# Gathering an expert's tokens as rows through a resting selection, then turning them, in a two-layer encoder with a mixture of experts

## The chip, the core and the metric

The kernel runs on one core of one Trainium2 chip. The metric is the device time of one execution in microseconds (us), which the chip itself measures. Three executions of the kernel before took 1951.26 to 1951.74 us, with a median of 1951.43 us. Lower is better.

## What is computed

The program is two encoder layers over 256 tokens of width 1024. Each layer has a mixer (retention, RWKV-7, latent attention) and a feed-forward block. The change lies in the second layer's feed-forward block, which is a mixture of eight experts where each token takes its two best ones:

```python
def swiglu(h, wg, wu, wd):
    return (jax.nn.silu(h @ wg) * (h @ wu)) @ wd

def moe_swiglu(h, router, wg, wu, wd):
    logits = (h @ router).astype(jnp.float32)
    top_v, top_i = lax.top_k(logits, TOP_K)          # TOP_K = 2
    top_w = jax.nn.softmax(top_v, axis=-1)
    comb = jnp.sum(jax.nn.one_hot(top_i, N_EXPERTS, dtype=jnp.float32) * top_w[..., None], axis=-2)
    out = jnp.zeros(h.shape, jnp.float32)
    for e in range(N_EXPERTS):                       # 8 experts, 1024 -> 3584 -> 1024
        out = out + comb[..., e:e + 1] * swiglu(h, wg[e], wu[e], wd[e]).astype(jnp.float32)
    return out.astype(h.dtype)
```

All inputs and weights are float32. `h` is the hidden state after an RMS norm with a gain per channel.

## The kernel before

**Items.** Each expert is worked off as one "item" of a hardware loop that all engines run in step, eight times here. An item takes at most 128 tokens: a 0/1 matrix `sel` (tokens x slots, two tiles of 128 tokens) picks them. Three weight matrices stream through a ring of three slots (`ring`, 2 MB each). A slot holds two halves, and a half is the unit of work; `q` counts the 42 halves of an item. Halves 0 to 27 are the gate and up matrices (`eg0`, `eu0`, ... `eg6`, `eu6`, two halves each), halves 28 to 41 the down matrix.

**Splitting.** To multiply float32 data at the speed of the rounded float32 type (fp32r), each operand is split in a high and a low part, and three products are summed. For each half the scalar engine (ACT) copies it from the ring into `w_hi` (L1003), the vector engine (DVE) subtracts that from the ring to give `w_lo` (L1677, a helper that all its two-input operations share), and TensorE (PE) does 12 matmuls of 128x128 by 128x512 (L1611). There are three buffers for such halves (PARTS), so ACT may begin half q only when PE has used up half q - 3. The order on each engine is the order of the code.

**Jobs and banks.** What PE writes goes to eight PSUM banks. The products of an item are a list, `ITEM`, with the engine that reads each one out. A job's bank is its place in that list modulo 8, and PE may begin a job only when the job eight places ahead of it in the list has been read out:

```python
def item_bank(job):
    k = ITEM_AT[job]
    if k >= BANKS:
        item_read_out(ITEM[k - BANKS][0])
```

In the list before, places 22 and 23 are `eg6` (read by ACT) and `eu6` (read by DVE), 24 and 25 are `eT5` and `eT6`, 26 and 27 are `gx0` and `gx1`, 28 and 29 are `ed0` and `ed1`. `ed0` and `ed1` are the two accumulators of the down matrix; PE asks for both banks just before half 28, behind `turn(5)`, four transposes of the activation (L1622). DVE reads `eu6` with one multiplication (`ehm`) that its code puts behind its work on half 29.

**The gather.** For each item the chosen tokens have to stand as columns, channel by channel, in `xg_hi` and `xg_lo`. PE makes them straight from the normed rows `hn` (two tiles of 128 tokens by 1024 channels), 16 full float32 matmuls of 128 columns with `hn` as the resting operand and `sel` moving (L1559), behind half 32, into `gx0` and `gx1`. ACT (L975) and DVE (L2167) scale and split them behind half 35, for the item that comes next. The first item's gather stands ahead of the loop, where it waits for `hn` and for `sel`, which DVE makes at the end of the routing (compare the logits, rank them, L1677 and its neighbours). After that come dummy products that keep PE busy, and the loop.

**GpSimd** (POOL) has nothing to do in this part but one load.

Of the kernel before, what the change touches and what calls it, by code (L numbers as in the profile page):

```python
# [11 lines left out]
F32 = mybir.dt.float32  # L12
I32 = mybir.dt.int32
ALU = mybir.AluOpType
# [3 lines left out]
P = 128  # L18
# [165 lines left out]
def moe_jobs():  # L184

    A, V = "act", "vec"
    out = [("eg0", A)] + [(f"sc{u}{t}", V) for u in range(2) for t in range(T)] + [("csT", A), ("eu0", V)]
    for j in range(1, 7):
        out += [(f"eg{j}", A), (f"eu{j}", V), (f"eT{j - 1}", V)]
    out += [("eT6", V), ("gx0", V), ("gx1", V), ("ed0", V), ("ed1", V)]  # L190
    return out


# [20 lines left out]
ITEM = moe_jobs()  # L214
ITEM_AT = {n: i for i, (n, _) in enumerate(ITEM)}
PANELS = panels()
AHEAD = 4
EP = 21
HALVES = 14 + 13
SURE = NE  # L220
# [34 lines left out]
class Signals:  # L255


    def __init__(self, nc):
        new = nc.alloc_semaphore
        self.ident_loaded = new("ident_loaded")  # L260
        self.const_loaded = new("const_loaded")
        self.pos_loaded = new("pos_loaded")
        self.mu_loaded = new("mu_loaded")
        self.vec_loaded = new("vec_loaded")
        self.first_gain_loaded = new("first_gain_loaded")
        self.gain_loaded = new("gain_loaded")
        self.router_loaded = new("router_loaded")
        self.fgain_loaded = new("fgain_loaded")
        self.i_hi_ready = new("i_hi_ready")
        self.i_lo_ready = new("i_lo_ready")  # L270
        self.i_half_used = new("i_half_used")
        self.i_x_hi_ready = new("i_x_hi_ready")
        self.i_x_lo_ready = new("i_x_lo_ready")
        self.f_hi_ready = new("f_hi_ready")
        self.f_lo_ready = new("f_lo_ready")
        self.f_half_used = new("f_half_used")
        self.f_x_hi_ready = new("f_x_hi_ready")
        self.f_x_lo_ready = new("f_x_lo_ready")
        self.hi_ready = new("hi_ready")
        self.lo_ready = new("lo_ready")  # L280
        self.half_used = new("half_used")
        self.x_hi_ready = new("x_hi_ready")
        self.product_ready = new("product_ready")
        self.freed_act = new("freed_act")
        self.freed_vec = new("freed_vec")
        self.act_step = new("act_step")
        self.vec_step = new("vec_step")
        self.pool_step = new("pool_step")
        self.out_stored = new("out_stored")
        self.angles_ready = new("angles_ready")  # L290
        self.trig_ready = new("trig_ready")
        self.sumsq_ready = new("sumsq_ready")
        self.var_ready = new("var_ready")
        self.root_ready = new("root_ready")
        self.factor_ready = new("factor_ready")
        self.hn_ready = new("hn_ready")
        self.shift_zero = new("shift_zero")
        self.xs_ready = new("xs_ready")
        self.lora_act_ready = new("lora_act_ready")
        self.knsq_ready = new("knsq_ready")  # L300
        self.knroot_ready = new("knroot_ready")
        self.decay_sig_ready = new("decay_sig_ready")
        self.rate_sig_ready = new("rate_sig_ready")
        self.logd_ready = new("logd_ready")
        self.exps_ready = new("exps_ready")
        self.cex_ready = new("cex_ready")
        self.scan_in_ready = new("scan_in_ready")
        self.rope_ready = new("rope_ready")
        self.silu_g_ready = new("silu_g_ready")
        self.gn_var_ready = new("gn_var_ready")  # L310
        self.gn_root_ready = new("gn_root_ready")
        self.ret_done = new("ret_done")
        self.qa_sumsq = new("qa_sumsq")
        self.qa_ready = new("qa_ready")
        self.mla_key_ready = new("mla_key_ready")
        self.masked_ready = new("masked_ready")
        self.prob_ready = new("prob_ready")
        self.merged_done = new("merged_done")
        self.blocks_ready = new("blocks_ready")
        self.x_ready = new("x_ready")  # L320
        self.state_ready = new("state_ready")
        self.rwkv_done = new("rwkv_done")
        self.y_pairs_done = new("y_pairs_done")
        self.route_exp = new("route_exp")
        self.route_diff = new("route_diff")
        self.mask_ready = new("mask_ready")
        self.items_ready = new("items_ready")
        self.sel_ready = new("sel_ready")
        self.ey_hi_ready = new("ey_hi_ready")
        self.fin_ready = new("fin_ready")  # L330
        self.items_done = new("items_done")


def build(nc, x, positions, attn_norm, w_in, rwkv_mu, rwkv_w0, rwkv_w2, rwkv_a0, rwkv_a2, rwkv_g2, rwkv_k_k,
# [5 lines left out]
    def sb(name, shape, dt=F32, where=None):  # L340
        size = -(-int(np.prod(shape[1:])) * 4 // 32) * 32
        if where is None:
            where = at[0]
            at[0] += size
        return nc.alloc_sbuf_tensor_at(name, shape, dt, offset=where)
# [93 lines left out]
    xg_lo = sb("xg_lo", [P, KD, P], F32R, where=X + 53248)  # L439
    ehT_hi = sb("ehT_hi", [P, 28, P], F32R, where=X + 57344)  # L440
    ehT_lo = sb("ehT_lo", [P, 28, P], F32R, where=X + 71680)
    sel = sb("sel", [P, T, P], where=X + 86016)
    weight = sb("weight", [P, 2, T], where=X + 87040)
    selT = sb("selT", [P, SEQ], F32R, where=X + 88064)
    ehm = sb("ehm", [P, 2, 512], where=X + 89088)
# [37 lines left out]
    freed = {"act": s.freed_act, "vec": s.freed_vec}  # L483
    FR = {e: freed_count(len(JOBS) - 1, e) for e in freed}
    IF = {e: item_freed(len(ITEM) - 1, e) for e in freed}
    LOOP_FR = {"act": FR["act"], "vec": FR["vec"] + AHEAD}
    NPAN = len(PANELS)

    def product(eng, job):
# [69 lines left out]
    def factor(m, t):  # L559

        return stat[:, 0, T * m + t:T * m + t + 1]
# [82 lines left out]
    def _(pool):  # L644
# [50 lines left out]
                own.step(G.tensor_copy(mk[:, t, :, 64:96], each(qa[:, t, 384:416], NH)), s.mla_key_ready)  # L695
        read_out(pool, "o11.1")
        pool.dma_start(fgain[:], final_norm.partition_broadcast(P)).then_inc(s.fgain_loaded, 16)


    @block.scalar  # L700
    def _(act):
# [28 lines left out]
        for l in range(DEPTH):  # L730
# [205 lines left out]
            if l:  # L936
                for t in range(T):
                    act.wait_ge(s.factor_ready, T * (2 * l + 1) + t + 1)
                    own.step(A.activation(hn[:, t, :], h[:, t, :], ACT.Copy, scale=factor(2 * l + 1, t)), s.hn_ready)
            if l == 0:  # L940
                for q in range(2, 36):
                    ffn_high(q)
# [24 lines left out]
        act.wait_ge(s.route_diff, 1)  # L967
        own.step(A.activation(stat[:, 6, 0:2], stat[:, 6, 0:2], ACT.Exp), s.route_exp)

        def gathered_hi(eng_wait):  # L970

            for u in range(2):
                b = eng_wait(f"gx{u}")
                for i in range(4):
                    ins = A.activation(xg_hi[:, 4 * u + i, :], b[:, i * P:(i + 1) * P], ACT.Copy,  # L975
                                       scale=gains[:, 1, 1, 4 * u + i:4 * u + i + 1])
                ins.then_inc(s.x_hi_ready, 1)

        def down_hi(eng_wait):

            for u in range(2):
                A.activation(ey_hi[:, 512 * u:512 * u + 512], eng_wait(f"ed{u}")[:], ACT.Copy)\
                    .then_inc(s.ey_hi_ready, 1)

        gathered_hi(lambda job: ahead(act, job))
        act.wait_ge(s.items_ready, 1)
        n_items = act.value_load(items[0:1, 24:25], min_val=SURE, max_val=SURE + 3)
        with act.Fori(0, n_items) as item:
# [16 lines left out]
            for q in range(2 * EP):  # L1005
# [11 lines left out]
                if q % 4 == 1 and 9 <= q <= 33:  # L1017
# [2 lines left out]
                                 item_product(f"eT{j}")[:].rearrange("p (c n) -> p c n", c=4),  # L1020
                                 ACT.Copy).then_inc(s.x_hi_ready, 1)
                if q == 35:
                    gathered_hi(item_product)
        def last_product(job):
            act.wait_ge(s.product_ready, n_items * len(ITEM) + (len(JOBS) + AHEAD + ITEM_AT[job] + 1 - len(ITEM)))
# [11 lines left out]
    def _(pe):  # L1037
# [514 lines left out]
        def gather(b_of):  # L1552

            for u in range(2):
                b = b_of(f"gx{u}")
                for i in range(4):
                    for t in range(T):
                        n = 4 * u + i
                        ins = M(b[:, i * P:(i + 1) * P], hn[:, t, n * P:n * P + P], sel[:, t, :], start=t == 0,  # L1559
                                stop=t == T - 1)  # L1560
                done(ins)

        keep_on(banks[ITEM_AT["gx0"] % BANKS], 4)
        pe.wait_ge(s.hn_ready, T)
        pe.wait_ge(s.sel_ready, 1)
        gather(lambda job: banks[ITEM_AT[job] % BANKS])
        for u in range(2):
            keep_on(banks[ITEM_AT[f"ed{u}"] % BANKS], 8)
            done(M(banks[ITEM_AT[f"ed{u}"] % BANKS][:], ident, cst[:, 0:512], start=True, stop=True))
# [14 lines left out]
        with pe.Fori(0, n_items) as item:  # L1584
# [41 lines left out]
            for j in range(7):  # L1626
                for g, name in enumerate(("eg", "eu")):
# [11 lines left out]
                    if j == g == 0:  # L1639
                        scatter(item, item_bank)  # L1640
                        b = item_bank("csT")
                        for t in range(T):
                            ins = TR(b[:, t * P:(t + 1) * P], sel[:, t, :], ident)
                        done(ins)
                if j:
                    turn(j - 1)
# [1 line left out]
            for j in range(7):  # L1648
# [3 lines left out]
                for r in range(2):  # L1652
# [11 lines left out]
                    if q == 32:  # L1664
                        pe.wait_ge(s.sel_ready, item + 2)
                        gather(item_bank)
        scatter(n_items, lambda job: banks[ITEM_AT[job] % BANKS])


    @block.vector  # L1670
    def _(dve):
# [517 lines left out]
        with dve.Fori(0, n_items) as item:  # L2189
# [19 lines left out]
            for q in range(2 * EP):  # L2209
# [16 lines left out]
                if q % 4 == 2 and 10 <= q <= 34:  # L2226
# [2 lines left out]
                    dve.wait_ge(s.x_hi_ready, item * 9 + (j + 3))  # L2229
                    tt(ehT_lo[:, 4 * j:4 * j + 4, :], b[:].rearrange("p (c n) -> p c n", c=4),  # L2230
                       ehT_hi[:, 4 * j:4 * j + 4, :].bitcast(F32), ALU.subtract).then_inc(s.freed_vec, 1)
                if q == 35:
                    gathered_lo(item_product, item * 9 + 9)

        def final(job):
# [48 lines left out]
```

## Time and profile before

| | value |
|---|---|
| median of the runs | 1951.43 us |
| the profiled execution's own time | 1948.17 us |
| its span, first to last instruction | 1946.4 us |
| routing, first gather, start of the loop | 925 to 943.5 us of the span |
| loop of 8 items | 943.5 to 1933 us, about 123.6 us each |
| TensorE busy over the span | 98% |
| mean granted TensorE clock | 0.996 |

The profiled execution took 1.8 us more than its span, and 3.3 us less than the median of the runs. Records of matmuls overlap (one begins before the last one's record ends), so PE's pace is read from the starts of its instructions or from the chain of work, and not from the length of one.

### The profile page before, as it was taken

Reading aid. Unit: us, or ns where it says so; the run is one execution under the profiler, and the core shown is the slowest. Engines: PE = TensorE matmul, PEld = TensorE weight load, DVE = VectorE, ACT = ScalarE, POOL = GpSimd, SP = SyncE. Lnnn points to the kernel's source line nnn. Section 1 sums busy time; section 2 is a strip of 40 time slices with the busy share of each in tenths; the row PEclk is TensorE's granted clock in tenths of the full one; section 3 lists DMA queues with packets and bytes.
Section 4 is the critical chain, followed back from the end, with each engine's and each line's share of the span. In section 5 each row is a group of like instructions: output and inputs, shape, how many; then the busy total and the mean of one; then the engine's idle time right before and its main releaser. Section 6 shows DMA issues by size and latency. Waiting matters only on the chain.

```text
span 1946.4 us, 25957 instructions
## 1 busy us (share of the span) xinstructions
PE 1903.1 (98%) x10058; PEld 1462.0 (75%) x10058; DVE 1356.4 (70%) x1403; ACT 1116.6 (57%) x1097; POOL 99.5 (5%) x124
## 2 busy tenths in 40 slices
PE   8999999999999999999999999999999999999997
PEld 7865655688888755654888888888888888888886
DVE  5664445444546644452888998889889899888997
ACT  5555211433444563110777777777777777777775
POOL 1340000000000520000000000000000000000000
PEclk9999999999999999999999999999999999999999
DMA  9542132553557422221899999999999999998994
GB/s 327 186 157 87 45 131 88 208 188 130 216 182 221 145 94 80 88 94 42 325 369 346 357 370 339 369 343 358 369 341 366 346 361 362 343 369 344 361 374 157
DMA packets 181498, 485.65 MB, mean 250 GB/s; under 512 B 5880, under 2 KB 12660, under 8 KB 172600
## 3 DMA queue, kind: packets, MB, share of 16 engines
q1 hardware_dynamic: 176256, 475.40, 67.0%
q0 software_dynamic: 1488, 5.57, 0.8%
q10 hardware_dynamic: 3688, 3.74, 0.7%
q8 instruction: 48, 0.79, 0.2%
q14 instruction: 18, 0.15, 0.0%
HBM read 479.93 MB, written 1.05 MB: 247 GB/s over the span
## 4 chain that ended last, share of the span: by engine, by line
PE 95%; DVE 2%; ACT 2%; issue 1%; DMA 0%; SPq 0%; ACTq 0%; DVEq 0%
PE bank L1611 47%; PE bank L1092 19%; PE bank L1205 9%; PE bank L1084 7%; PE bank L1559 2%; PE bank L1255 1%; PE bank L1622 1%; PE bank L1580 1%; PE bank L1304 1%; DVE m L1677 1%; DMA ring<-w_in_dram 0%; PE bank L1281 0%; PE bank L1229 0%; PE bank L1171 0%; PE bank L1269 0%
## 5 line engine op out<-in xcount | busy, mean ns | idle before, releaser
L1677 DVE TENSOR_TENSOR w_lo<-ring,w_hi 128x2048 fp32r<-128x2048 f32 x336 | 765.1, 2290 | 112.4 <-ACT w_hi L1003 112.4
L1003 ACT ACTIVATE w_hi<-ring 128x2048 fp32r<-128x2048 f32 x336 | 643.7, 1916 | 126.3 <-PE bank L1611 126.2
L1611 PE MATMUL bank<-w_hi,xg_hi 128*128 128x512 f32 x896 | 353.0, 394 | 1.5 <-DVE w_lo L1677 1.5
L1611 PE MATMUL bank<-w_hi,xg_lo 128*128 128x512 f32 x896 | 349.7, 390 | 0.0
L1611 PE MATMUL bank<-w_lo,xg_hi 128*128 128x512 f32 x896 | 349.4, 390 | 0.0
L1611 PEld LDWEIGHTS bank<-w_hi,xg_hi 128*128 128x128 f32 x896 | 168.8, 188 | 36.1 <-DVE w_lo L1677 2.3
L1611 PEld LDWEIGHTS bank<-w_hi,xg_lo 128*128 128x128 f32 x896 | 168.2, 188 | 35.3
L1611 PEld LDWEIGHTS bank<-w_lo,xg_hi 128*128 128x128 f32 x896 | 168.4, 188 | 34.0
L1205 PE MATMUL bank<-ring,hnT 128*128 128x512 f32 x384 | 178.4, 600 | 0.0
L1611 PE MATMUL bank<-w_hi,ehT_hi 128*128 128x512 f32 x448 | 176.5, 394 | 0.0
L1611 PE MATMUL bank<-w_hi,ehT_lo 128*128 128x512 f32 x448 | 174.8, 390 | 0.0
L1611 PE MATMUL bank<-w_lo,ehT_hi 128*128 128x512 f32 x448 | 174.5, 390 | 0.0
L1677 DVE TENSOR_TENSOR ring_lo<-ring,f_hi 128x2048 fp32r<-128x2048 f32 (+1 forms) x36 | 75.4, 2111 | 76.6 <-ACT f_hi L922 76.6
L1677 DVE TENSOR_TENSOR ring_lo<-ring,i_hi 128x2048 fp32r<-128x2048 f32 (+2 forms) x36 | 79.6, 2219 | 68.0 <-ACT i_hi L743 68.0
L1205 PEld LDWEIGHTS bank<-ring,hnT 128*128 128x128 f32 x384 | 69.4, 190 | 63.9 <-issue 61.3
L1092 PE MATMUL bank<-i_hi,ix_hi 128*128 128x512 f32 (+2 forms) x288 | 110.3, 383 | 4.9 <-DVE ring_lo L1677 3.8
L1092 PE MATMUL bank<-ring_lo,ix_hi 128*128 128x512 f32 (+2 forms) x288 | 111.0, 385 | 0.0
L1092 PE MATMUL bank<-i_hi,ix_lo 128*128 128x512 f32 (+2 forms) x288 | 109.4, 380 | 0.0
L1611 PEld LDWEIGHTS bank<-w_hi,ehT_lo 128*128 128x128 f32 x448 | 84.1, 188 | 17.7
L1611 PEld LDWEIGHTS bank<-w_hi,ehT_hi 128*128 128x128 f32 x448 | 84.4, 188 | 16.8
L1611 PEld LDWEIGHTS bank<-w_lo,ehT_hi 128*128 128x128 f32 x448 | 84.2, 188 | 16.9
L1084 PE MATMUL bank<-ring,yT 128*128 128x512 f32 x192 | 85.5, 598 | 3.0 <-issue 3.0
(401 smaller groups left out, 2532.7 us busy)
## 6 DMA issues: line engine op xcount, KB each, us to landing
ring<-moe_w_gate_dram SPq DMA_DIRECT2D x56, 2048.0 KB, 7.8
ring<-moe_w_up_dram SPq DMA_DIRECT2D x56, 2048.0 KB, 8.0
ring<-moe_w_down_dram SPq DMA_DIRECT2D x56, 2048.0 KB, 8.4
ring<-w_in_dram SPq DMA_DIRECT2D x26, 2048.0 KB, 8.6
ring<-w_branch_dram SPq DMA_DIRECT2D x6, 2048.0 KB, 8.2
ring<-ffn_w_gate_dram SPq DMA_DIRECT2D x5, 2048.0 KB, 8.3
ring<-ffn_w_up_dram SPq DMA_DIRECT2D x5, 2048.0 KB, 8.1
ring<-ffn_w_down_dram SPq DMA_DIRECT2D x5, 2048.0 KB, 8.0
```

The costliest lines, as they stand in the source:

```text
L1003: A.activation(w_hi[:, q % PARTS, :], ring[:, i, o:o + HALF], ACT.Copy).then_inc(s.hi_ready, 1)
L1084: ins = M(b[:, 0:width], lhs[:, c, t * P:(t + 1) * P], w[:, c, c0:c0 + width], start=c == 0, stop=c == k - 1)
L1092: ins = M(dst, a[:, c, tok], v[:, cols], start=start and n == 0, stop=stop and n == 2, skip_group_check=True)
L1205: ins = M(dst[:], hnT[:, c, (g % 2) * P:(g % 2) * P + P], gates[0][:, 512 * c:512 * c + 512], start=c == 0, stop=c == KD - 1, skip_group_c ...
L1255: ins = M(b[ch, cols], left[ch, :], right[ch, :], start=True, stop=True)
L1304: ins = M(b[:, 256 * i:256 * i + 256], C("same_block"), rows_of[:, 2 * u + i, :], start=True, stop=True)
L1559: ins = M(b[:, i * P:(i + 1) * P], hn[:, t, n * P:n * P + P], sel[:, t, :], start=t == 0, stop=t == T - 1)
L1580: ins = M(b[:], selT[:, t * P:(t + 1) * P], part[:, 512 * u:512 * u + 512], start=i == 0, stop=i == 1)
L1611: ins = M(dst, a, w, start=start and n == 0, stop=stop and n == 2, skip_group_check=True)
L1622: ins = TR(b[:, c * P:(c + 1) * P], ehm[:, j % 2, c:512:4], ident)
L1677: return V.tensor_tensor(out_, a, b, op)
```

## The change

The selection becomes the resting operand and the token rows move. `hn` is split once ahead of the loop: ACT writes `hn_hi` (rounded to fp32r) beside `hn`, and POOL subtracts to give `hn_lo`. A gather is now 8 fp32r matmuls of 512 columns into two new jobs, `gy0` and `gy1`; ACT copies them to SBUF as rows (`xrow`); and behind half 35 PE turns them by 8 transposes of 128x128 into `gx0` and `gx1`. ACT's and DVE's scaling and splitting moves from half 35 to half 38. The list of jobs has 32 places in place of 30.

```diff
@@ moe_jobs
-    out += [("eT6", V), ("gx0", V), ("gx1", V), ("ed0", V), ("ed1", V)]
+    out += [("eT6", V), ("gy0", A), ("gy1", A), ("gx0", V), ("gx1", V), ("ed0", V), ("ed1", V)]
...
-AHEAD = 4
+AHEAD = 6
...
-    sel = sb("sel", [P, T, P], where=X + 86016)
+    sel = sb("sel", [P, T, P], F32R, where=X + 86016)
+    hn_lo = sb("hn_lo", [P, T, D], F32R, where=hn_at)
+    hn_hi = sb("hn_hi", [P, T, D], F32R, where=X + 113664)
+    xrow = sb("xrow", [P, D], where=X + 121856)
...
-    LOOP_FR = {"act": FR["act"], "vec": FR["vec"] + AHEAD}
+    LOOP_FR = {"act": FR["act"] + 2, "vec": FR["vec"] + AHEAD - 2}
@@ gpsimd, at its end
         pool.dma_start(fgain[:], final_norm.partition_broadcast(P)).then_inc(s.fgain_loaded, 16)
+        for t in range(T):
+            pool.wait_ge(s.hn_ready, 2 * t + 2)
+            G.tensor_tensor(hn_lo[:, t, :], hn[:, t, :], hn_hi[:, t, :].bitcast(F32), ALU.subtract)\
+                .then_inc(s.hn_lo_ready, 1)
@@ scalar
                     own.step(A.activation(hn[:, t, :], h[:, t, :], ACT.Copy, scale=factor(2 * l + 1, t)), s.hn_ready)
+                    own.step(A.activation(hn_hi[:, t, :], h[:, t, :], ACT.Copy, scale=factor(2 * l + 1, t)), s.hn_ready)
...
+        def gathered_rows(eng_wait):
+
+            for u in range(2):
+                A.activation(xrow[:, 512 * u:512 * u + 512], eng_wait(f"gy{u}")[:], ACT.Copy).then_inc(s.freed_act, 1)
+
...
+        gathered_rows(lambda job: ahead(act, job))
         gathered_hi(lambda job: ahead(act, job))
...
                 if q == 35:
+                    gathered_rows(item_product)
+                if q == 38:
                     gathered_hi(item_product)
@@ tensor
         def gather(b_of):
 
             for u in range(2):
+                b = b_of(f"gy{u}")
+                for t in range(T):
+                    for part in (hn_hi, hn_lo):
+                        ins = M(b[:], sel[:, t, :], part[:, t, 512 * u:512 * u + 512], start=t == 0 and part is hn_hi,
+                                stop=t == 1 and part is hn_lo)
+                done(ins)
+
+        def turn_gathered(b_of):
+
+            for u in range(2):
                 b = b_of(f"gx{u}")
                 for i in range(4):
-                    for t in range(T):
-                        n = 4 * u + i
-                        ins = M(b[:, i * P:(i + 1) * P], hn[:, t, n * P:n * P + P], sel[:, t, :], start=t == 0,
-                                stop=t == T - 1)
+                    n = 4 * u + i
+                    ins = TR(b[:, i * P:(i + 1) * P], xrow[:, n * P:n * P + P], ident)
                 done(ins)
 
-        keep_on(banks[ITEM_AT["gx0"] % BANKS], 4)
-        pe.wait_ge(s.hn_ready, T)
+        keep_on(banks[ITEM_AT["gy0"] % BANKS], 4)
+        pe.wait_ge(s.hn_lo_ready, T)
         pe.wait_ge(s.sel_ready, 1)
         gather(lambda job: banks[ITEM_AT[job] % BANKS])
+        pe.wait_ge(s.freed_act, LOOP_FR["act"])
+        turn_gathered(lambda job: banks[ITEM_AT[job] % BANKS])
...
                     if q == 32:
                         pe.wait_ge(s.sel_ready, item + 2)
                         gather(item_bank)
+                    if q == 35:
+                        item_read_out("gy1")
+                        turn_gathered(item_bank)
@@ vector
-                if q == 35:
+                if q == 38:
                     gathered_lo(item_product, item * 9 + 9)
```

**PE's program between halves 27 and 28, in the loop.** The rows below are PE's instructions in order: the end of `eu6` (in bank 7), the turn of `eT5` (in bank 0), and the first products of half 28. A register row carries the wait of the line of code behind it. Before:

```order
L1611 MATMUL bank7<-w_hi_127,xg_lo_130 128x512
L1588 REGISTER_ALU [waits freed_vec]
L1622 MATMUL bank0<-cst_56,ehm_136 128x128 [waits freed_act]
L1622 MATMUL bank0<-cst_56,ehm_136 128x128 x3
L1588 REGISTER_ALU [waits freed_vec]
L1615 REGISTER_ALU [waits freed_vec]
L1611 MATMUL bank4<-w_hi_127,ehT_hi_131 128x512 [waits lo_ready]
```

And now:

```order
L1639 MATMUL bank7<-w_hi_127,xg_lo_130 128x512
L1616 REGISTER_ALU [waits freed_vec]
L1650 MATMUL bank0<-cst_56,ehm_139 128x128 [waits freed_act]
L1650 MATMUL bank0<-cst_56,ehm_139 128x128 x3
L1616 REGISTER_ALU [waits freed_act]
L1643 REGISTER_ALU [waits freed_vec]
L1639 MATMUL bank6<-w_hi_127,ehT_hi_131 128x512 [waits lo_ready]
```

The down accumulators moved from banks 4 and 5 to banks 6 and 7, the banks of `eg6` and `eu6`; what is waited for there was `eu5` and `eT4`, and is now `eg6` and `eu6`.

**ACT's program ahead of the loop.** The rows are those from the norm of the last layer to the first gathered tokens, with `h` the hidden state. Before, two rows stood between the second square root and the routing's exponential, L939 `hn<-h,stat` twice. Now:

```order
L721 ACTIVATE stat<-stat 128x1 [waits var_ready]
L948 ACTIVATE hn<-h,stat 128x1024 [waits factor_ready]
L949 ACTIVATE hn_hi<-h,stat 128x1024
L948 ACTIVATE hn<-h,stat 128x1024 [waits factor_ready]
L949 ACTIVATE hn_hi<-h,stat 128x1024
L978 ACT_TABLE_LOAD
L978 ACTIVATE stat<-stat 128x2 [waits route_diff]
L983 ACTIVATE xrow<-bank 128x512 [waits product_ready] x2
L990 ACTIVATE xg_hi<-bank,gains 128x128 [waits product_ready]
```

Two copies of 1024 columns came in beside `hn`, and two of 512 columns ahead of `xg_hi`. POOL's new row, `L705 TENSOR_TENSOR hn_lo<-hn,hn_hi 128x1024 [waits hn_ready] x2`, is the last of its program.

## Rows read from the trace of the kernel before

**Rows 1.** The page: TensorE's busy time, share of span, instructions
```profile
PE 1903.1 (98%) x10058; PEld 1462.0 (75%) x10058; DVE 1356.4 (70%) x1403; ACT 1116.6 (57%) x1097; POOL 99.5 (5%) x124
```

**Rows 2.** Windows: us, each engine's busy us, PEclk, DMA share, GB/s
```profile
1062.00:1186.00 124.00, 124.00 (x577) 103.60 (x576) 110.07 (x76) 93.88 (x70) 0.00 (x0) 1.00 0.96 357
```

**Rows 3.** Waits from 950 to 1940: us in total, times, longest
```profile
ACT w_hi L1003 <- PE bank L1611: 125.4, 214, 1.6
...
PE bank L1580 <- DVE ey_lo L1677: 0.2, 1, 0.2
```

**Rows 4.** Chain that ended last, in order: start us, us, what
```profile
1024.64 0.47 PE bank L1622 x4
...
1148.24 0.47 PE bank L1622 x4
...
1154.67 8.22 PE bank L1611 x36
1162.89 3.57 PE bank L1559 x32
...
1196.41 1.82 PE bank L1580 x8
```

**Rows 5.** Timeline around half 28: start us, us, engine, instruction
```profile
1145.27 4.53 DVE L1677 TENSOR_TENSOR w_lo<-ring,w_hi 128x2048 fp32r<-128x2048 f32 x2 [0.40 <-ACT w_hi L1003]
...
1145.55 1.92 ACT L1003 ACTIVATE w_hi<-ring 128x2048 fp32r<-128x2048 f32 x1 [0.32 <-PE bank L1611]
...
1148.46 0.48 PE L1611 MATMUL bank<-w_hi,ehT_hi 128*128 128x512 f32 x1
1148.74 0.60 ACT L1019 ACTIVATE ehT_hi<-bank 128x512 fp32r<-128x512 f32 x1 [1.27 <-PE bank L1622]
...
1149.71 0.68 DVE L1677 TENSOR_TENSOR ehm<-bank,esg 128x512 f32<-128x512 f32 x1
```

**Rows 6.** Timeline behind half 35, the split of the gathered tokens
```profile
1164.75 1.12 ACT L975 ACTIVATE xg_hi<-bank,gains 128x128 fp32r<-128x128 f32 x4
...
1167.16 2.16 DVE L2167 SCALAR_TENSOR_TENSOR xg_lo<-bank,gains,xg_hi 128x128 fp32r<-128x128 f32 x8
```

**Rows 7.** Timeline ahead of the loop: routing, first gather, first half
```profile
925.38 2.17 ACT L939 ACTIVATE hn<-h,stat 128x1024 f32<-128x1024 f32 x2
...
927.66 0.29 DVE L1677 TENSOR_TENSOR higher<-rt 128x128 f32<-128x128 f32 x1
...
928.19 0.29 DVE L1677 TENSOR_TENSOR equal<-equal,cst 128x128 f32<-128x128 f32 x1
...
932.27 0.28 DVE L2113 TENSOR_SCALAR sel<-cst,spos 128x128 f32<-128x128 f32 x1
...
932.94 3.74 PE L1559 MATMUL bank<-sel,hn 128*128 128x128 f32 x32
...
936.71 1.14 ACT L975 ACTIVATE xg_hi<-bank,gains 128x128 fp32r<-128x128 f32 x4 [0.64 <-PE bank L1559]
...
943.46 0.50 PE L1611 MATMUL bank<-w_hi,xg_hi 128*128 128x512 f32 x1 [1.49 <-DVE w_lo L1677]
```

**Rows 8.** Timelines of POOL's and DVE's two-input operations in the mixer
```profile
81.63 2.78 POOL L657 TENSOR_TENSOR rope_tmp<-raw,cosT 128x256 f32<-128x256 f32 x1
...
83.73 1.76 DVE L1677 TENSOR_TENSOR prev<-prev,pr 128x1024 f32<-128x1024 f32 x1
...
91.17 0.74 POOL L656 TENSOR_TENSOR rope_tmp<-raw,cosT 128x256 f32<-128x256 f32 x1
...
134.97 0.46 POOL L655 TENSOR_TENSOR mrope_tmp<-mq,sinT 128x128 f32<-128x128 f32 x1
...
147.51 1.22 DVE L1677 TENSOR_TENSOR tmp<-y_ret 128x1024 f32<-128x1024 f32 x1
```

**Rows 9.** Windows with a lower granted clock, columns as above
```profile
925.00:930.00 5.00, 4.77 (x29) 4.77 (x30) 2.71 (x16) 3.56 (x4) 0.00 (x0) 0.68 1.00 357
...
1934.00:1938.00 4.00, 1.18 (x4) 0.65 (x4) 2.73 (x5) 1.86 (x4) 0.00 (x0) 0.89 0.00 0
```

More of the change, by code:

```diff
@@ L296, in __init__ @@
         self.hn_ready = new("hn_ready")
+        self.hn_lo_ready = new("hn_lo_ready")
         self.shift_zero = new("shift_zero")
@@ L441, in build @@
     ehT_lo = sb("ehT_lo", [P, 28, P], F32R, where=X + 71680)
-    sel = sb("sel", [P, T, P], where=X + 86016)
+    sel = sb("sel", [P, T, P], F32R, where=X + 86016)
+    hn_lo = sb("hn_lo", [P, T, D], F32R, where=hn_at)
+    hn_hi = sb("hn_hi", [P, T, D], F32R, where=X + 113664)
+    xrow = sb("xrow", [P, D], where=X + 121856)
+    assert X + 125952 <= int(nc.sbuf_usable_end)
     weight = sb("weight", [P, 2, T], where=X + 87040)
@@ L1642, in _ @@
                         for t in range(T):
-                            ins = TR(b[:, t * P:(t + 1) * P], sel[:, t, :], ident)
+                            ins = TR(b[:, t * P:(t + 1) * P], sel[:, t, :].bitcast(F32), ident)
                         done(ins)
```

## The prediction

> **What bounds the kernel now.** I read the page first: TensorE (PE) is busy for 98% of the span [rows 1]. Then the windows of the loop: in an item of 124 us PE is busy for all of it, DVE for 110 and ACT for 94, the clock is full, and the DMA engines are 0.96 busy [rows 2]. Busy PE alone proves little, so the table of waits comes next: over the eight items ACT waits 125 us for PE to free a split buffer, and PE itself waits once, for 0.2 us [rows 3]. So the loop goes at PE's pace, and what PE does in an item counts in full, eight times. The chain of work prices it: from one turn of `eT5` to the same one an item later it is 1148.24 - 1024.64 = 123.6 us; 36 products of 512 columns take 8.22 us, or 0.228 each; 8 such products of another kind take 1.82; a turn of four transposes takes 0.47; and the gather, 32 passes for 16 float32 matmuls, takes 3.57 [rows 4].
>
> **The change, part by part.**
>
> *The gather and its turn, in the loop.* 3.57 us go [rows 4]. In their place stand 8 fp32r products of 512 columns, 8 x 0.228 = 1.82 us, which is what the eight scatter products take [rows 4], and 8 transposes. Two turns would be 2 x 0.47 = 0.94; I count 0.86, as one of the two changes from and to fp32r is saved. Together 2.68, so PE has 0.89 us less to do per item, 7.1 us in eight. The bounds are 0.8 (0.94 for the turns) and 1.0 (0.09 per transpose).
>
> *The copies and the moved split.* ACT gets two copies of 512 columns from PSUM per item, 0.60 each [rows 5]. It has 30 us of idle time in 124 [rows 2], and the copies stand behind half 35, where PE is three halves away from needing what comes next. I cost them at nothing. The split at half 38: ACT's 2 x 1.12 us and DVE's 2.16 [rows 6] now start behind fewer microseconds of PE work, because the gather no longer follows them. Count from E, PE's end of half 35. ACT's half 38 is done at E + 2.1 and its part of the split at E + 4.4; DVE ends half 38 at 4.4, its split at 6.6 and the low part of half 39 at 8.9. PE wants that after the turn and three halves of 12 products, 0.86 + 3 x 2.73 = 9.05. It is hidden, by 0.15 us only; if it is late by 0.3, that is 2.4 us in all.
>
> *The banks of the down accumulators.* This is the part of the diff that nothing in its arithmetic tells of. With two more places in the list, `ed0` and `ed1` stand in the banks of `eg6` and `eu6`. Before, PE started half 28 at 1148.46, right behind its turn [rows 5]. Now it has to wait until DVE has read `eu6`. DVE does that in its own order: halves 28 and 29 first, from 1145.27 to 1149.80, and then `ehm`, which runs from 1149.71 to 1150.39 [rows 5]. Neither moves forward, since ACT's copy of half 29 starts at 1145.55 only when PE has ended half 26, and DVE's part of half 29 (2.3 us) stands behind it. So PE restarts at about 1150.39 + 0.1 = 1150.5 in place of 1148.46: 2.05 us of idle PE in every item, 16.4 us in eight. Queued behind this wait is the rest of PE's item. ACT and DVE find their buffers freed 2 us later, but they wait for PE anyway [rows 3], and nothing is won back. The 0.89 us of the gather lies elsewhere in PE's row and covers none of it. Bounds: 1.9 (no latency) and 2.3 (a slow restart), 15.2 to 18.4 in all.
>
> *Ahead of the loop, POOL's subtractions.* ACT now does four passes of 1.09 us where it did two in 2.17 [rows 7], so the first `hn_hi` is there at about 927.6 and the second at 929.7. POOL then subtracts 1024 columns twice. Its two-input operation takes 0.74 us for 256 columns and 0.46 for 128 [rows 8], 2.2 ns a column, which gives an estimate of 2.4 us for 1024. The two together would be over by 932.5 if POOL were alone, before `sel` is there at 932.55 [rows 7]. It isn't alone. In the mixer POOL's 0.74 us operation takes 2.78, and DVE's operation of 1.22 takes 1.76, when they meet [rows 8]: one waits for the other's end, in turns. Here POOL's first subtraction begins at about 927.9, between DVE's `higher` at 927.66 and the two comparisons behind it [rows 7]. DVE's next waits until 930.3 and is over at 930.6; POOL's second then goes first and ends at 933.0; only then comes the operation that before stood at 928.19. The rest of the routing, and so `sel` and the first gather, come 933.0 - 928.2 = 4.8 us later. Bounds: 0, if they don't meet, and 5.6, if POOL needs 2.8 each (four times 0.70 between starts).
>
> That is a row's reading. The Trainium skill says the same by rule ("SBUF — State Buffer", "Who interferes with whom"): a vector instruction with two SBUF inputs contends with a GpSimd one that reads SBUF, and the one that comes first holds the shared ports for its whole length. By that rule the delay is the full two subtractions; without it the sum would be 4.8 us less. This rule speaks against the change, as the split looks as if it had an idle engine to itself.
>
> *The first gather.* Before, from its start at 932.94 to ACT's end of `xg_hi` at 936.71 + 1.14 = 937.85 it is 4.9 us [rows 7]. Now: products 1.9 to 2.0, ACT's second copy to 2.65, first turn to 3.3, ACT's 2 x 1.12 to 5.55. The order copies, turn, split is serial here, with nothing to cover it: 0.7 us more. PE's clock is the third price. The granted clock was 0.68 on the mean of 925 to 930, so 64% of that stretch was at the lower level of 1.2 GHz, and 0.89 from 1934 to 1938, where PE had work for 1.2 of 4 us [rows 9]. A routing that is 4.8 us longer leaves PE idle by that much behind its dummy products; at half speed the 8 products and 8 transposes would cost 2.7 us more. I take 1.0, and 0 and 2.7 as ends. ACT's first half follows `xg_hi`, DVE's follows that, and PE starts the loop on it, at 943.46 before [rows 7], so all of this comes through: 4.8 + 0.7 + 1.0 = 6.5.
>
> **The sum.** -7.1 + 16.4 + 6.5 = +15.8 us. The profiled execution's 1948.17 becomes 1964.0 (its span 1962.2). The runs' median lies 3.3 us above it, and by the same difference it becomes 1951.43 + 15.8 = 1967.2.
>
> **The rivals.**
> - *POOL and DVE don't meet, or only briefly.* For it: the operations of the routing are 0.3 us long, with gaps between them, and none that short stands in rows 8. Then 4.8 and the clock's 1.0 fall away: -7.1 + 16.4 + 0.7 = +10.0, 1961.4 us.
> - *The read-out of `eu6` is not late.* If DVE took `ehm` before it touched half 29, PE would not wait in the loop, and the gather's gain would stand against what lies ahead of it: -7.1 + 6.5 = -0.6, 1950.8 us, no change. Against it: the order of DVE's rows in all eight items.
> - *Faster, by one mechanism: the gather's saving is seen because the wait falls inside the turn.* The place is the wait ahead of half 28, and its price decides: with 0.7 ahead of the loop the change is even at (7.1 - 0.7) / 8 = 0.8 us per item, and with a wait of nothing it is -6.4, 1945.0 us. For that `ehm` would have to end by 1149.2 where it ends at 1150.39 [rows 5].
> - *More is lost: the split at half 38 makes half 39 late, or the slow clock lasts into the loop.* 2.4 us for the one, some 3 for the other: 1970 to 1974 us.
>
> **How the numbers follow.** Chances: the forecast 0.60, POOL hidden 0.20, more lost 0.12, the wait absent 0.05, faster 0.03. The bounds of the forecast's own terms give 1951.43 + (15.2 - 8.0 + 0 + 0.7 + 0) = 1959.3 at the low end and 1951.43 + (18.4 - 6.4 + 5.6 + 0.7 + 2.7) = 1972.4 at the high one. From 1959.5 to 1972.5 holds the forecast, POOL hidden and a part of the last, and leaves out less than 2 in 10. A measurement of this kernel can tell some 0.2%, 4 us, from no change. Slower by more than that: 0.60 + 0.20 + 0.12 = 0.92; within it 0.05; faster 0.03.
>
> **What the profile after would show.** In each item PE stands still for about 2 us ahead of half 28, put down to DVE's `ehm`, a wait that isn't there now; if it is missing, the largest term is wrong. The period of an item is 123.6 - 0.9 + 2.05 = 124.8 us. The gather is 8 products in 1.8 us, the turn 8 transposes in 0.9. Ahead of the loop the second `higher`/`equal` operation of DVE shows a length of 2 us and more, beside POOL's first subtraction; the first gather starts near 938 in place of 932.9, and the loop's first product near 950. If the gather starts before 934, POOL was hidden. If PE waits for DVE's `w_lo` at half 39, the moved split was not free. The prediction is wrong as a whole if the period of an item is below 123.6.

## The result, and the profile after

The changed kernel takes 1975.32 us, median of four runs from 1973.97 to 1977.16. The kernel before took 1951.35 beside it, median of four. The ratio is 1.0123 (95% interval 1.0111 to 1.0136): 24 us slower. I had said 1967.2, from 1959.5 to 1972.5, so the direction was right and the size too small, outside the range. In the profiled executions the spans are 1946.4 and 1973.9 us, 27.5 apart; the sums below are made against that pair, since their parts are read from the two traces. The medians are only 24.0 apart: the profiled execution of the kernel before lies 3.2 us below its median, that of the changed kernel 0.4 above. Which part of the program makes up those 3.2 us no trace shows.

The page's first part and its clock row:

```profile
PE 1911.5 (97%) x9914; PEld 1462.1 (74%) x9914; DVE 1358.9 (69%) x1403; ACT 1125.5 (57%) x1117; POOL 104.2 (5%) x126
```

Beside [rows 1] PE has 144 instructions fewer and yet 8 us more of busy time. Fewer instructions that take longer point to the clock. Of the table of waits, 950 to 1960 us, three rows (the first has its match in [rows 3], the others have none):

```profile
ACT w_hi L1019 <- PE bank L1639: 146.6, 207, 4.0
...
PE bank L1639 <- DVE ehm L1708: 14.5, 8, 1.8
...
PE bank L1639 <- DVE w_lo L1708: 2.1, 1, 2.1
```

PE now waits for DVE's `ehm`, eight times. (The row of `w_lo` is the start of the loop, which the window of [rows 3] left out; it is 2.08 us long, where before it was 1.49.) The longest wait of ACT for PE grew from 1.6 to 4.0 us, so there is a place in the loop where PE gets on much later than before. The chain of work finds it. The second item's rows are these, with the start in us, the length and the work:

```profile
1158.90 0.69 DVE ehm L1708
1159.71 7.36 PE bank L1639 x24
1167.07 0.47 PE bank L1650 x4
...
1175.75 1.88 PE bank L1576 x8
1177.63 8.16 PE bank L1639 x36
1185.80 0.87 PE bank L1586 x8
...
1285.34 0.70 DVE ehm L1708
1286.04 0.12 issue
1286.16 5.75 PE bank L1639 x24
```

The gather is 8 products in 1.88 us and the turn 0.87, 2.75 together where [rows 4] has 3.57: 0.82 us won. The two halves behind the wait, 24 products, take 7.36 us. In the next item they take 5.75. Of the eight items seven show 7.35 to 7.37, and one 5.75. The windows around the first item's wait say why (us, busy time of PE, PEld, DVE, ACT and POOL, then the granted clock, DMA share and GB/s):

```profile
1032.00:1033.00 1.00, 0.00 (x0) 0.00 (x0) 1.00 (x2) 1.00 (x2) 0.00 (x0) 1.00 1.15 492
1033.00:1034.00 1.00, 0.74 (x2) 0.63 (x3) 0.22 (x2) 0.88 (x1) 0.00 (x0) 0.77 0.92 393
1034.00:1035.00 1.00, 1.00 (x4) 0.76 (x3) 1.00 (x1) 0.00 (x0) 0.00 (x0) 0.50 0.99 377
1035.00:1036.00 1.00, 1.00 (x4) 0.81 (x3) 1.00 (x1) 0.00 (x0) 0.00 (x0) 0.50 1.02 410
1036.00:1037.00 1.00, 1.00 (x3) 0.75 (x3) 1.00 (x6) 0.00 (x0) 0.00 (x0) 0.52 0.74 295
1037.00:1038.00 1.00, 1.00 (x6) 0.81 (x5) 0.31 (x1) 0.09 (x1) 0.00 (x0) 1.00 1.15 459
```

PE idles, and just as it starts again its clock falls to the 1.2 GHz level and stays there for some 3.4 us. PE's own timeline there has the wait and the slow products, 0.43 us from start to start where the products ahead of the wait and from 1037 us on have 0.23:

```profile
1030.81 0.63 PE L1650 MATMUL bank<-cst,ehm 128*128 128x128 f32 x4
1033.26 0.56 PE L1639 MATMUL bank<-w_hi,ehT_hi 128*128 128x512 f32 x1 [1.82 <-DVE ehm L1708]
1033.62 0.63 PE L1639 MATMUL bank<-w_lo,ehT_hi 128*128 128x512 f32 x1
1034.05 0.63 PE L1639 MATMUL bank<-w_hi,ehT_lo 128*128 128x512 f32 x1
```

From the turn to the first product it is 2.45 us. In the kernel before the turn's row is

```profile
1148.08 0.63 PE L1622 MATMUL bank<-cst,ehm 128*128 128x128 f32 x4
```

and the product starts at 1148.46 [rows 5], 0.38 us later: 2.07 us of waiting. Ahead of the loop the timeline now reads:

```profile
924.85 1.13 ACT L948 ACTIVATE hn<-h,stat 128x1024 f32<-128x1024 f32 x1
...
927.11 4.72 POOL L705 TENSOR_TENSOR hn_lo<-hn,hn_hi 128x1024 fp32r<-128x1024 f32 x2 [4.36 <-ACT hn_hi L949]
...
928.53 1.09 DVE L1708 TENSOR_TENSOR higher<-rt 128x128 f32<-128x128 f32 x1
...
929.55 2.43 DVE L1708 TENSOR_TENSOR equal<-rt 128x128 f32<-128x128 f32 x1
932.01 0.29 DVE L1708 TENSOR_TENSOR equal<-equal,cst 128x128 f32<-128x128 f32 x1
...
949.81 0.50 PE L1639 MATMUL bank<-w_hi,xg_hi 128*128 128x512 f32 x1 [2.08 <-DVE w_lo L1708]
```

Two DVE operations of 0.29 us [rows 7] last 1.09 and 2.43, and end when one of POOL's subtractions does (2.36 us each). The loop starts at 949.81 in place of 943.46, 6.35 us later.

Not all of this is POOL's. Three stretches of PE's work ahead of the loop run slower, and the granted clock is 0.50 over 925 to 930 and over 935 to 940. In the chain of the changed kernel they are the products of the logits, the dummies ahead of the first gather, and the gather:

```profile
924.70 3.60 PE bank L1555 x16
...
935.20 2.04 PE bank L1117 x8
937.24 3.43 PE bank L1576 x8
```

In the chain of the kernel before the first two are

```profile
925.23 2.18 PE bank L1537 x16
...
931.97 1.13 PE bank L1099 x8
```

The slow products of the logits are no sure effect of the change: the changed kernel and e4 below have the same program up to here, and e4's trace shows 1.97 us for them.

### The profile page after: what moved, and what is told of

Read it like the earlier page. It is cut to its first block, busy times and chain, and to the rows that moved or that the text cites. A ratio compares the mean times of both kernels' runs of the same rounds, so it can differ in the third digit from the quotient of the medians.

```text
span 1973.9 us, 25723 instructions
## 1 busy us (share of the span) xinstructions
PE 1911.5 (97%) x9914; PEld 1462.1 (74%) x9914; DVE 1358.9 (69%) x1403; ACT 1125.5 (57%) x1117; POOL 104.2 (5%) x126
## 4 chain that ended last, share of the span: by engine, by line
PE 93%; DVE 3%; ACT 2%; issue 1%; DMA 0%; SPq 0%; DVEq 0%; ACTq 0%
PE bank L1639 47%; PE bank L1110 19%; PE bank L1223 9%; PE bank L1102 7%; PE bank L1273 1%; PE bank L1650 1%; PE bank L1576 1%; PE bank L1608 1%; PE bank L1322 1%; DVE m L1708 1%; DMA ring<-w_in_dram 0%; PE bank L1586 0%; PE bank L1299 0%; PE bank L1247 0%; PE bank L1189 0%
## 5 line engine op out<-in xcount | busy, mean ns | idle before, releaser
L1639 PE MATMUL bank<-w_hi,ehT_hi 128*128 128x512 f32 x448 | 181.1, 404 | 14.5 <-DVE ehm L1708 14.5
L1639 PE MATMUL bank<-w_lo,ehT_hi 128*128 128x512 f32 x448 | 179.3, 400 | 0.0
L1639 PE MATMUL bank<-w_hi,ehT_lo 128*128 128x512 f32 x448 | 179.0, 400 | 0.0
```

The source lines that it names most:

```text
L1639: ins = M(dst, a, w, start=start and n == 0, stop=stop and n == 2, skip_group_check=True)
```

## The experiments

Theory A was that the moved banks cost a wait of 2.07 us and, behind it, 1.6 us of slow clock in most items, and that POOL's reads cost the rest ahead of the loop. Its rivals for the loop: the turn, the copies or the split at half 38 (B), a slow clock with another source (C), the DMA engines (D). The kernel before ran beside them with medians of 1950.67 us (first four) and 1950.90 us (last three).

**e1: the banks put back.**

```diff
+ITEM_BANK = {n: i % BANKS for n, i in ITEM_AT.items()}
+ITEM_BANK.update({"gx0": 6, "gx1": 7, "ed0": 4, "ed1": 5})
```

with every bank of an item's job, and the job whose read-out it waits for, taken from that table.

> The changed kernel with one thing undone: the down accumulators stand in banks 4 and 5 again, as before the change, and gx0 and gx1 take 6 and 7, so that half 28 waits for the readers of eu5 and eT4 and not of eg6 and eu6. All the rest of the change stays. Theory A (the bank wait costs 2.07 us per item, and behind it half-speed products cost 1.6 us more in 7 of 8 items): 16.6 + 11.3 us come back, 1947.4 us, and the item's period is 122.8 us. Rival B (the loss lies in the turn, in ACT's copies or in the split at half 38): 1970 us or more, period near 126.

1950.77 us, ratio to before 1.0004 (0.9995 to 1.0013). 24.5 us come back from a change of four bank numbers, and B falls. Its chain has no wait ahead of half 28, and items last 1527.66 - 1404.89 = 122.77 us where nothing is late. It stands 3.4 us above what I expected. Its own trace has a slow stretch at the start of the loop, 1.6 us, and in two items, which last 0.8 us longer, a thing that the trace of the kernel before doesn't show, ACT waiting for weights:

```profile
951.57 7.36 PE bank L1642 x24
...
1183.66 10.27 DMA ring<-moe_w_gate_dram
...
1199.61 5.78 PE bank L1642 x24
...
1404.89 5.50 PE bank L1642 x24
...
1527.66 5.49 PE bank L1642 x24
```

The slow stretch stands behind an idle one: PE waits 2.08 us for `w_lo` ahead of the loop's first product. The same wait of 2.08 to 2.09 us stands in the changed kernel and in e3, e4, e5 and e6. The 24 products behind it take 5.74 us in the changed kernel and 5.76 in e3, but 7.29 to 7.37 in e1, e4, e5 and e6. In the kernel before, e2 and e7 the wait is 1.49 us and the products take 5.73 to 5.78.

**e2: the kernel before, with the banks alone moved.**

```diff
+ITEM_BANK.update({"ed0": 6, "ed1": 7})
```

> The kernel before with nothing of the change but the banks: ed0 and ed1 in banks 6 and 7, behind eg6 and eu6. The gather is the old one. Theory A: PE stands still 2.07 us ahead of half 28 and then runs at 1.2 GHz for a while, 2.07 + 1.6 us per item, 1951.4 + 25 to 30 = 1976 to 1981 us. Rival B: 1951 to 1953 us. A rival C, that the wait costs only itself and the slow clock has another source in the change: 1951.4 + 16.6 = 1968 us.

1970.33 us, 1.0107 (1.0091 to 1.0122): 19.7 us slower, without a line of the new gather. That is between what A and C give. In its trace all eight items have the wait, with the same 14.5 us in the table of waits, and the slow products come in two of the eight (7.36 and 7.34 us for the 24, the others 5.72 to 5.75). The profiled execution agrees to a tenth: 8 x 2.07 + 2 x 1.62 = 19.8 against 1967.86 - 1948.17 = 19.7 us. So the wait always costs itself, and whether the clock falls behind it differs from item to item. I had expected nearly all to fall, and that part of A was too strong. That slow products stand here at all, without the new gather, already speaks against C. Why the clock falls in seven items of one trace and in two of the other, behind the same wait, no run shows.

```profile
1403.12 0.69 DVE ehm L1680
...
1403.93 7.36 PE bank L1614 x24
```

**e3: the changed kernel, PE kept busy in the wait.**

```diff
-            b0, b1 = item_bank("ed0"), item_bank("ed1")
+            b0 = item_bank("ed0")
+            keep_on(b0, 8)
+            b1 = item_bank("ed1")
```

> The changed kernel, with 8 dummy products of 128x128 (some 1.9 us) into bank 6 between PE's wait for eg6 and its wait for eu6, so that PE works through most of the 2.07 us. The wait itself stays. Theory A, with the clock as its second half: the granted clock stays at full, the 11.3 us of slow products vanish, the 16.6 us stay: 1964 us. If the slow products come from something else than PE's idle stretch: 1975 us. If the dummies reach beyond the wait: some us more than 1964.

1967.40 us, 1.0086 (1.0073 to 1.0100). It stands 3.4 us above the 1964 that I expected. Half 28 starts as late as in the changed kernel, at 1033.14, 2.45 us behind the turn, but PE worked until then (each dummy product counts as two in the row), and the 24 products take 5.72 to 5.75 us in all eight items:

```profile
1030.69 0.63 PE L1650 MATMUL bank<-cst,ehm 128*128 128x128 f32 x4
1031.15 1.95 PE L1117 MATMUL bank<-cst 128*128 128x128 f32 x16
...
1033.14 0.49 PE L1639 MATMUL bank<-w_hi,ehT_hi 128*128 128x512 f32 x1
1033.47 0.39 PE L1639 MATMUL bank<-w_lo,ehT_hi 128*128 128x512 f32 x1
```

The idle stretch is what makes the clock fall, and C is out. In the profiled executions the dummies save 1975.70 - 1964.16 = 11.5 us, seven times 1.62 is 11.3. The medians differ by less, 7.9 us, and come from separate comparisons. The profiled execution of the changed kernel lies at its median; that of e3 is the fastest of its five, 3.2 us below theirs. So something costs e3's other runs a few us that its trace doesn't have. What it is stays open; a slow start of the loop as in e1 would be 1.6 of it.

**e4: the changed kernel, with `ehm` of `eu6` ahead of half 29 on DVE.**

```diff
-                if q % 4 == 1 and 5 <= q <= 29:
-                    j = (q - 5) // 4
+                if q % 4 == 1 and 5 <= q <= 25 or q == 28:
+                    j = (q - 5) // 4 if q < 28 else 6
```

> The changed kernel with DVE's ehm for eu6 put ahead of its work on half 29 and not behind it. The banks are those of the change. PE then waits only for its own last product and the 0.68 us of ehm, less the turn: about 0.7 us per item in place of 2.07. Theory A: 11 us of waiting come back, and all of the slow clock if so short a wait leaves it alone: 1953 us; 1964 us if the clock still falls. Rival B: 1975 us.

1956.02 us, 1.0026 (1.0016 to 1.0036), 3 us above the 1953 that I expected; 1.6 of them are the slow start of the loop (24 products in 7.37 us). From turn to half 28 it is 1.11 us, so 0.73 of waiting, and behind it the clock stays up in all eight items (5.75 for the 24). Against e1 it costs 5.3 us; 8 x 0.73 is 5.8. The banks need not move back if the reader is early, and so the delay was DVE's order behind the bank, as the prediction had it.

```profile
1032.85 0.63 PE L1650 MATMUL bank<-cst,ehm 128*128 128x128 f32 x4
1033.96 0.49 PE L1639 MATMUL bank<-w_hi,ehT_hi 128*128 128x512 f32 x1 [0.48 <-DVE ehm L1708]
```

**e5: e1, with POOL writing and not reading.**

```diff
-            G.tensor_tensor(hn_lo[:, t, :], hn[:, t, :], hn_hi[:, t, :].bitcast(F32), ALU.subtract)\
-                .then_inc(s.hn_lo_ready, 1)
+            G.memset(hn_lo[:, t, :].bitcast(F32), 0.0).then_inc(s.hn_lo_ready, 1)
```

> The first experiment's kernel (banks back), and POOL fills hn_lo with zeros by a memset in place of the two subtractions, so that it reads nothing from SBUF. This leaves the low part of the gathered tokens out of the computation; every other instruction stays. Theory A (POOL's reads hold back two of DVE's routing operations by 2.3 us each, and PE's longer idle stretch halves its clock in the first gather): 4.1 us of delay and about 2.5 us of slow products go, 1950.8 - 6.6 = about 1944. If the loss ahead of the loop lies in the order of copy, turn and split instead: no change from 1950.8.

The low part of the gathered rows is left out of the computation here. 1946.42 us, 0.9976 (0.9967 to 0.9985), 4.4 us less than e1 where I had said 6.6; its trace still has one slow stretch at the start of the loop (24 products in 7.29 us) and one late transfer. With POOL's memsets alongside, DVE's operations keep their 0.28 to 0.29 us, also the two that run while a memset does:

```profile
929.75 0.29 DVE L1710 TENSOR_TENSOR equal<-equal,cst 128x128 f32<-128x128 f32 x1
929.85 0.96 POOL L707 MEMSET hn_lo<- 128x1024 f32 x1 [1.12 <-ACT hn_hi L950]
930.08 0.29 DVE L1710 TENSOR_TENSOR higher<-higher,equal 128x128 f32<-128x128 f32 x1
```

In e1 the same two last 2.32 and 2.31 us, beside the subtractions. It was POOL's reading, and not POOL's being there. This trace also has the first gather at full clock (8 products in 1.87 us): from its start to the loop's first product it is 945.85 - 934.60 = 11.25 us, where the kernel before had 10.52. That is the price of copy, turn and split in a row, 0.73.

**e6: e1, with more dummy work ahead of the routing's mask.**

```diff
-        keep_on(b, 6)
+        keep_on(b, 16)
```

> The first experiment's kernel with 16 dummy products in place of 6 ahead of PE's wait for the routing's mask, some 2.3 us more, so that PE is idle there for 2 us and not for 4. POOL's subtractions stay. If the clock ahead of the loop costs what I hold against it: 1.5 to 3 us less than the first experiment, about 1948.5. If PE's clock there hangs on something else: 1950.8.

1947.89 us, 0.9984 (0.9975 to 0.9993): 2.9 us less than e1, with POOL's subtractions in place (DVE's two held-back operations last 2.45 and 2.43). The granted clock of 930 to 935 is 0.92 where e1 had 0.50, and of 935 to 940 it is 0.76 where e1 had 0.50. PE's products on the routing's mask (which tokens each expert takes) and the dummies behind them run at full speed again (the dummies take 1.13 us, in e1 2.05), but the gather itself hardly does:

```profile
936.37 1.13 PE bank L1119 x8
937.50 3.20 PE bank L1578 x8
```

It takes 3.20 us for e1's 3.43. So the longer routing cost twice, its own length and the clock of the work behind it, and the dummies gave back the part ahead of the gather. The loop starts 1.7 us earlier than in e1's trace.

**e7: the version the findings point to.** On top of e1, the first item's gather is the old one; ACT makes `hn_hi` behind the exponential; POOL subtracts only when DVE's routing is done, into a buffer of its own:

```diff
-    hn_lo = sb("hn_lo", [P, T, D], F32R, where=hn_at)
+    hn_lo = sb("hn_lo", [P, T, D], F32R, where=hnT_at)
...
+            pool.wait_ge(s.half_used, HALVES)
             G.tensor_tensor(hn_lo[:, t, :], hn[:, t, :], hn_hi[:, t, :].bitcast(F32), ALU.subtract)\
...
-        gather(lambda job: banks[ITEM_BANK[job]])
-        pe.wait_ge(s.freed_act, LOOP_FR["act"])
-        turn_gathered(lambda job: banks[ITEM_BANK[job]])
+                    ins = M(b[:, i * P:(i + 1) * P], hn[:, t, n * P:n * P + P], sel[:, t, :].bitcast(F32),
+                            start=t == 0, stop=t == T - 1)
```

> The version that the findings point to: banks back; the first item's gather is the old one in full float32 straight from hn, with no row copies and no turn; ACT makes hn_hi behind the routing's exponential, and POOL subtracts into a buffer of its own only when DVE's routing is over. Items 2 to 8 gather the new way. Theory A: nothing is lost ahead of the loop, and 0.82 us are won in each of eight items, 1950.7 - 6.6 = 1944, perhaps 1 to 2 us above that where a transfer of weights is now late. Rival D (the faster loop runs into the DMA engines, so that the gain is given back): 1948 or more.

1944.26 us, 0.9967 (0.9955 to 0.9980): faster than the kernel before by 6.6 us. That is 8 x 0.82, but the interval holds all from 3.9 to 8.8 us, so the closeness proves nothing. The loop starts at 943.51, POOL's two subtractions run from 935.60 to 940.27 beside operations of DVE that keep their length, and an item lasts 1271.75 - 1148.98 = 122.77 us:

```profile
1148.98 5.50 PE bank L1649 x24
...
1163.16 1.88 PE bank L1579 x8
...
1173.20 0.87 PE bank L1589 x8
...
1271.75 5.49 PE bank L1649 x24
```

D shows in one item of its trace, where a transfer of gate weights took 10.47 us and ACT waited 1.28 for it; that item lasts 1.0 us longer than the others. Such late transfers are on the chain of every trace whose items last 122.77 us, one or two in e5, e7 and e1 and four in e6, and on none of the slower ones (the kernel before, the changed one, e2, e3, e4). In e6's profiled execution, the slowest of its 11 runs, they add up to 2.8 us. So a part of what is won is given back: the DMA engines are 0.96 busy over the loop.

## Why the prediction was right and wrong

*What bounds the kernel, and the gather in the loop: right.* PE sets the pace, and 0.82 us per item were won for the 0.89 said, 6.6 us for 7.1. e7 shows the gain by itself. The copies on ACT and the split at half 38 cost nothing that can be seen; PE's one wait for `w_lo`, 2.1 us, is the start of the loop and not half 39.

*The banks: the wait was right, its price was not.* 2.07 us per item against 2.05, with the engine, instruction and place as named. What failed is the step "2.05 us of idle PE in every item, 16.4 us in eight", with its bounds of 1.9 and 2.3: it took an idle stretch to cost its own length. Behind it PE's clock fell, in seven of eight items of the trace, for 1.62 us each, 11.3 in all. The prediction priced the clock ahead of the loop, on [rows 9], and did not ask the same at the other place where it had itself put an idle stretch of 2 us; the rival "more is lost" gave it some 3 us. e3 shows the term, and e2 that it comes in some items and not in others, which also makes a range of it: from 0 to 8 x 1.62 = 13 us. With that the upper end would have been beyond 1980. What decides it from item to item stays open.

*Ahead of the loop: right in sum by luck, mixed in its parts.* 6.35 us against 6.5. POOL's subtraction takes 2.36 us for the estimated 2.4, and DVE's operations wait for it in turns as said; that is 3.0 us in this trace and 4.1 in e1's, for the 4.8 said, because POOL's had already run for a while when DVE's came (1.4 us here, 0.3 in e1). PE feels 0.6 less of it, which the prediction left out: in the kernel before, PE's dummy products held its products on the mask until 929.97, when DVE had made the mask by 929.33:

```profile
929.16 0.17 DVE L2088 TENSOR_SCALAR rt<-rt 128x16 f32<-128x16 f32 x1
...
929.97 0.41 PE L1544 MATMUL bank<-rt,cst 128*128 128x8 f32 x2
```

The serial order of the first gather costs 0.7, as said (e5). The clock costs 3.3 where I took 1.0 and had 2.7 as the upper end: 0.9 in the products of the logits (3.60 us for 2.18, less a start that is 0.5 earlier), 0.7 in the dummies ahead of the first gather and 1.7 from its start to the loop (12.9 us for e5's 11.25), where the 8 products took 3.43 us for 1.9. So the clock cost 2.3 more than said and POOL 2.4 less, and the two happened to cancel. By the rule of the Trainium skill cited in the prediction ("SBUF — State Buffer", "Who interferes with whom"), a vector operation with two SBUF inputs contends with a GpSimd operation that reads SBUF, and not with one that only writes it. The trace agrees: DVE's operations of 0.29 us last up to 2.43 beside the subtractions, and 0.29 beside the memsets of e5.

*The sum.* 16.6 of waiting, 11.3 of slow clock, 6.35 ahead of the loop, less 6.6: 27.7, and the spans differ by 27.5. The forecast had 16.4, nothing, 6.5 and 7.1. The medians are 24.0 apart, so against them the same sum is 3.7 too much. The experiments agree as far as they reach: 24.5 us in medians go with the banks (e1), where its trace has 1.6 for a slow start of the loop and 1.6 for late transfers against it, and e5 and e6 find some 4 and 3 us ahead of the loop, which are not to be added, since the clock is in both.

## What to carry to other kernels

Where a list's places decide the buffers (place modulo the number of banks), two new entries move every later entry to another bank and so to another reader to wait for: print that pairing before and after, and ask for each wait what its reader has queued ahead of it. And price an idle stretch of TensorE as its length plus what the clock may take behind it (here 2.07 and 0 or 1.62 us), at each place where one appears; dummy products in the wait, or a reader that is a little earlier, took that second half away here. Work given to an idle GpSimd was not free here where it read SBUF while VectorE was on the path with two SBUF inputs: operations of 0.29 us lasted up to 2.45.

## What the runs showed of the hardware

PE's clock fell behind idle stretches of 2.07 us in a stream that was full on both sides, in 7 of 8 items of one trace and in 2 of 8 of another with the same wait (e2), and behind none of the eight stretches of 0.73 us (e4). Ahead of the loop, behind a wait of 2.08 us, it fell in four traces of six (e1, e4, e5, e6), and behind one of 1.49 us in none of three (the kernel before, e2, e7). In the loop's first item of the changed kernel it fell as PE started again, at the start of the loop in e6 some 1.5 us later. Products of 512 columns then took 0.43 us in place of 0.23, for about 3.4 us. Of two kernels that differ in nothing but 8 dummy products per item, the one that does more work was faster, by 7.9 us in medians of separate comparisons.
